# A two-block transformer kernel: nine steps of its hand-written order and bank assignment are moved

## The reference

```python
def first_block(x, ...):
    # layer A: chunked gated linear attention (GLA), 4 heads
    proj = rmsnorm(h) @ a_w_in                  # q 512, k 512, v 1024, gate 1024, glr 16
    gk = log_sigmoid(glr @ w_gk2 + b_gk) / 16
    bcum = cumsum(gk) in chunks of 64
    q_t, k_t, k_dec = q*exp(bcum), k*exp(-bcum), k*exp(b_last - bcum)
    h = h + (norm(tril(q_t @ k_t.T) @ v + q_t @ S) * silu(gate)) @ a_w_out
    h = h + relu(rmsnorm(h) @ w_up)**2 @ w_down      # 1024 -> 4096 -> 1024
    # layer B: sliding window attention, 16 query heads, 2 key heads, window 128
    h = h + swa(rmsnorm(h) @ b_w_q, rmsnorm(h) @ w_kv, bias = rel_table[bucket], sinks) @ b_w_out
    h = h + relu(rmsnorm(h) @ w_up)**2 @ w_down
    return rmsnorm(h, ln_final)

def second_block(x, p, ...):
    z = rmsnorm(x) @ w_in            # qa, ka, va, qb, kb, vb, gates ga, gb
    y_a = rope_attention(qa, ka, va) @ w_out_a
    y_b = dilated_attention(qb, kb, vb, rel_bias) @ w_out_b
    x = x + (sigmoid(ga + b) * y_a + sigmoid(gb + b) * y_b) @ w_out
    x = x + relu(rmsnorm(x) @ w_ff1)**2 @ w_ff2
    x = x + sigmoid(rmsnorm(x) @ w_ple_gate) * (p @ w_ple)
    return rmsnorm(x)
```

## Time and profile before

| | |
|---|---|
| time, median of 3 runs | 1019.68 us (1018.61 to 1027.45) |
| the profiled execution | 1019.38 us, of which the span of instructions is 1017.6 us |
| mean granted clock of TensorE | 0.993 |
| busy: PE, DVE, ACT, POOL | 990.9, 672.9, 492.8, 29.9 us |
| moved by DMA | 177.29 MB, 174 GB/s on average |

### The profile page before, as it was taken

The page is one execution under the profiler, slowest core; times in us unless marked ns, Lnnn a source line. Parts: engine busy times, 40 slices in busy tenths (PEclk is TensorE's granted clock), DMA queues, the critical chain, the costliest instruction groups (busy, mean ns, idle before and its releaser), DMA issues.

```text
span 1017.6 us, 13016 instructions
## 1 busy us (share of the span) xinstructions
PE 990.9 (97%) x5404; PEld 837.4 (82%) x5404; DVE 672.9 (66%) x931; ACT 492.8 (48%) x584; POOL 29.9 (3%) x56
## 2 busy tenths in 40 slices
PE   8989999999999999999999999999999999999997
PEld 7776888888888777888888889878878788888886
DVE  4765866656656985765656658975756585656665
ACT  4353444444445774544444455346553453444453
POOL 1000100000000000000000012000000000000001
PEclk9989999999999999999999999999999999999999
DMA  6752569655563325995455565344166465455551
GB/s 194 225 192 83 165 157 256 208 182 191 202 212 124 125 87 142 243 290 178 166 193 182 206 206 165 128 143 145 44 201 209 158 224 190 166 173 199 186 187 42
DMA packets 113100, 177.29 MB, mean 174 GB/s; under 512 B 4563, under 2 KB 75615, under 8 KB 113040
## 3 DMA queue, kind: packets, MB, share of 16 engines
q1 hardware_dynamic: 113040, 176.44, 55.0%
HBM read 174.60 MB, written 1.83 MB: 173 GB/s over the span
## 4 chain that ended last, share of the span: by engine, by line
PE 82%; DVE 9%; ACT 3%; DMA 3%; issue 1%; POOL 1%; SPq 1%; POOLq 0%; DVEq 0%; ACTq 0%
PE ps L285 79%; PE ps L289 3%; DVE wlo L1080 3%; DMA raw<-in_a_w_in 3%; DVE M L1088 2%; ACT M L1919 1%; DVE M L1080 1%; ACT whi L1922 1%; SPq L2600 1%; POOL st L2494 1%; DVE cc L1685 1%; DVE RR L1088 0%; DMA M<-in_ln_mix 0%; ACT M L1922 0%; DVE st L1641 0%
## 5 line engine op out<-in xcount | busy, mean ns | idle before, releaser
L285 PE MATMUL ps<-whi,RR 128*128 128x512 f32 (+1 forms) x1552 | 401.4, 390 | 1.6 <-DVE RR L1080 1.3
L1080 DVE TENSOR_TENSOR wlo<-raw,whi 128x1024 fp32r<-128x1024 f32 (+1 forms) x322 | 372.6, 1199 | 30.4 <-ACT whi L1922 30.0
L1922 ACT ACTIVATE whi<-raw 128x2048 fp32r<-128x2048 f32 (+2 forms) x162 | 302.6, 1871 | 179.3 <-PE ps L285 129.0
L285 PEld LDWEIGHTS ps<-whi,RR 128*128 128x128 f32 x1552 | 284.5, 189 | 61.5 <-issue 5.1
L285 PE MATMUL ps<-RR,whi 128*128 128x512 f32 (+1 forms) x1264 | 262.7, 352 | 5.3 <-DVE RR L1088 3.5
L285 PEld LDWEIGHTS ps<-RR,whi 128*128 128x128 f32 x1264 | 201.2, 190 | 34.2 <-issue 4.6
L285 PE MATMUL ps<-wlo,RR 128*128 128x512 f32 (+1 forms) x776 | 221.3, 387 | 0.9 <-DVE wlo L1080 0.9
L285 PEld LDWEIGHTS ps<-wlo,RR 128*128 128x128 f32 x776 | 144.3, 189 | 31.5 <-DVE wlo L1080 1.7
L1080 DVE TENSOR_TENSOR M<-M,ps 128x512 f32<-128x512 f32 x56 | 38.3, 686 | 168.1 <-ACT M L1922 164.7
L285 PEld LDWEIGHTS ps<-RR,wlo 128*128 128x128 f32 (+1 forms) x1016 | 138.5, 190 | 9.3 <-DVE wlo L1080 0.7
L285 PE MATMUL ps<-RR,wlo 128*128 128x256 f32 (+1 forms) x1016 | 144.9, 282 | 0.0
(11 more groups left out here) (94 smaller groups left out, 374.7 us busy)
## 6 DMA issues: line engine op xcount, KB each, us to landing
raw<-in_w_up SPq DMA_DIRECT2D x32, 1024.0 KB, 5.3
raw<-in_w_down SPq DMA_DIRECT2D x32, 1024.0 KB, 5.0
raw<-in_w_ff SPq DMA_DIRECT2D x32, 1024.0 KB, 5.2
raw<-in_w_in SPq DMA_DIRECT2D x23, 1024.0 KB, 5.2
raw<-in_a_w_in SPq DMA_DIRECT2D x11, 1024.0 KB, 8.4
raw<-in_a_w_out SPq DMA_DIRECT2D x4, 1024.0 KB, 5.0
raw<-in_b_w_q SPq DMA_DIRECT2D x4, 1024.0 KB, 5.0
raw<-in_b_w_out SPq DMA_DIRECT2D x4, 1024.0 KB, 5.0
```

The costliest lines, as they stand in the source:

```text
L285: return pe.matmul(out, lhsT, rhs, start=start, stop=stop, skip_group_check=True)
L1080: return dve.tensor_tensor(out, a, b, op)
L1922: return act.activation(out, in_, ACT.Copy, **k)
```

## The change

Nine places of the hand-written order are altered; the set of results is the same.

1. Start: PE warms up with 9 small products instead of 4, x's first half is transposed before the gain's transpose, which goes to bank 0, and its second half after five more warm-up products. SP loads the identity before x. ACT makes a small copy first, so its table is loaded ahead.
2. Bias rows: `line(i)` makes one bias row (on PE a product, on DVE its copy), and it is called from inside `gates()`: row 0 after gate 0, row 1 after gate 1, rows 2 and 3 after the next two steps. The stores of SP stay where they are.
3. `gates()` on DVE no longer yields between `kt` and `kd`, so `kd` comes before the low part of the next block.
4. The transposes of norm 2's quarters 0 and 1 take banks 4 and 5 instead of the next `misc()` banks.
5. `rows_scale(2)` is called before the key half, and the low part of a block (`take()`) before the copy of the scales on DVE.
6. In `window()` the low parts come before the shares.
7. The call of `early()` is also made at step 6 of the output projection, and `gemm_up` takes the bank pair of its second block when it reaches that block.
8. The tile `pT` takes bank 3.
9. On ACT the sigmoids of `SA` come after the rounding of the weights of `gemm_b(1024, 2)`.

```diff
--- before.py
+++ after.py
@@ -371,34 +371,30 @@
                 t = mm(b[:, i, T:2 * T], lo[:, k, 128 * i:128 * i + 128], hT[0][:, k, :], False, k == 7)
             return t
 
+
         blocks = []
         for f in range(0, n, 256):
             j, hi, lo = block(w[:, c0 + f:c0 + f + 256], 8, 256)
             tile = name + (f,)
             take(tile, *misc_pair())
-            blocks.append((tile, K.pair(tile, 512), j, hi, lo))
+            b = K.pair(tile, 512)
+            blocks.append((tile, b, j, hi, lo))
+            for i in range(2):
+                t = part(b, i, j, hi, lo, range(4) if hook else range(8))
+                if i == 0:
+                    if hook and f == 0:
+                        hook()
+                    yield
             if not hook:
-                for i in range(2):
-                    t = part(*blocks[-1][1:2], i, j, hi, lo, range(8))
-                    if i == 0:
-                        yield
                 t.then_inc(*K.filled(tile))
                 K.value["w_used", j] = K.full(tile)
                 yield
-        if hook:
-
-            for n_, (tile, b, j, hi, lo) in enumerate(blocks):
-                for i in range(2):
-                    part(b, i, j, hi, lo, range(4))
-                    if n_ == 0 and i == 0:
-                        hook()
-                        yield
-            for tile, b, j, hi, lo in blocks:
-                for i in range(2):
-                    t = part(b, i, j, hi, lo, range(4, 8))
-                t.then_inc(*K.filled(tile))
-                K.value["w_used", j] = K.full(tile)
-                yield
+        for tile, b, j, hi, lo in blocks if hook else []:
+            for i in range(2):
+                t = part(b, i, j, hi, lo, range(4, 8))
+            t.then_inc(*K.filled(tile))
+            K.value["w_used", j] = K.full(tile)
+            yield
 
     def gemm_b(name, w, c0, n, xT, ready, pairs=None):
 
@@ -435,7 +431,7 @@
 
     def norm_turn(s, k2):
         tile = ("nt", s, k2)
-        b = take(tile, 2 * (k2 - 2) if s in (1, 2, 3, 5) and k2 > 1 else misc())
+        b = take(tile, 2 * (k2 - 2) if s in (1, 2, 3, 5) and k2 > 1 else 4 + k2 if s == 2 else misc())
         for j in range(2):
             k = 2 * k2 + j
             for c in range(2):
@@ -546,14 +542,16 @@
         for _ in range(n):
             mm(K.banks[:, 3, 0:128], V.S["ones"][:, :], V.S["ones"][:, :], True, True)
 
-    spin(4)
+    spin(9)
+    norm_early(0)
     tile = ("g", 0)
-    b = take(tile, misc())
+    b = take(tile, 0)
     for w in due(K.dma("id"), K.dma("g0")):
         pe.wait_ge(*w)
     tr(b[:, 0:16], V.M[0:16, 0:128]).then_inc(*K.filled(tile))
     spin(5)
-    norm_rest(0)
+    for k2 in (2, 3):
+        norm_turn(0, k2)
 
 
 
@@ -576,7 +574,9 @@
     tr(b[:, 0:60], V.M[0:60, 15000:15128]).then_inc(*K.filled(tile))
 
     tab, sel = V.S["tab"], V.S["sel"]
-    for i in range(4):
+
+    def line(i):
+
         tile = ("br", i)
         b = take(tile, misc())
         for w in due(K.dma("tab", 1), K.at("tab_end"), K.dma("sel")):
@@ -597,8 +597,11 @@
                 h = 2 * h2 + j
                 t = mm(b[:, j * 256:j * 256 + 256], V.S["gk2"][:, h * 128:h * 128 + 128], V.glr, True, True)
             t.then_inc(*K.filled(tile))
-            yield
-        for _ in range(4):
+            line(h2)
+            yield
+        for i in range(4):
+            if i < 2:
+                line(2 + i)
             yield
         while count["qk"] < 4:
             yield
@@ -728,8 +731,8 @@
     t = q_part(1, range(4, 8))
     t.then_inc(*K.filled(("q2",)))
     K.value["w_used", jq] = K.full(("q2",))
+    rows_scale(2)
     kv_part(0, range(4, 8)).then_inc(*K.filled(("kk",)))
-    rows_scale(2)
     kv_part(1, range(4, 8)).then_inc(*K.filled(("vt",)))
     K.value["w_used", jk] = K.full(("vt",))
 
@@ -1033,7 +1036,7 @@
     project("po", A["w_out_2"][0], 5, "ty", lambda: turn_parts("ty", V.SB, 1, K.at("mix", 512)), V.tyT)
 
     pT = oB
-    b = take(("pT",), misc())
+    b = take(("pT",), 3)
     for w in due(K.dma("p")):
         pe.wait_ge(*w)
     for j in range(2):
@@ -1361,11 +1364,13 @@
                 t = ts(bc[:, h * 256:h * 256 + 256], K.bank(tile)[:, j * 256:j * 256 + 256], G[:, 64 + h:65 + h], None,
                        ALU.add, None)
             t.then_inc(*K.emptied(tile))
+            line(h2)
             yield
         for w in due(K.empty(("gate", 0)), K.empty(("gate", 1))):
             dve.wait_ge(*w)
         stt(e1, bc, -1.0, bc, ALU.mult, ALU.max).then_inc(*K.up("g_abs"))
         low = step(ts(bc, bc, 0.0, None, ALU.min, None))
+        line(2)
         yield
         for w in due(K.at("g_ln"), low):
             dve.wait_ge(*w)
@@ -1373,6 +1378,7 @@
         for w in due(d):
             dve.wait_ge(*w)
         d = step(ts(e1, e1, 1.0 / 16.0, None, ALU.mult, None))
+        line(3)
         yield
         for w in due(d, K.at("scan_one")):
             dve.wait_ge(*w)
@@ -1517,6 +1523,7 @@
     squares(2, *xs_free(2), *all_x(K, 2))
     kv_lows(2, 3)
     diagonals(2)
+    take()
     for w in due(K.full(("rbt", 2))):
         dve.wait_ge(*w)
     dve.tensor_copy(RB[:, 0:256], K.bank(("rbt", 2))[:, 0:256]).then_inc(*K.emptied(("rbt", 2)))
@@ -1527,7 +1534,6 @@
             t = tt(V.KT[64 * half:64 * half + 64, g, :], K.bank(("kk",))[64 * g:64 * g + 64, 0:256],
                    RB[64 * g:64 * g + 64, 0:256], ALU.mult)
     t.then_inc(*K.emptied(("kk",)))
-    take()
 
     def cc(p):
         return S["cc"][:, 32 * (p % 3):32 * (p % 3) + 32]
@@ -1576,10 +1582,10 @@
         for i in range(11):
             if i < 8:
                 soft(i)
+            if 3 <= i:
+                lows(i - 3)
             if 0 < i < 9:
                 shares(i - 1)
-            if 3 <= i:
-                lows(i - 3)
             yield
 
     def halves(n):
@@ -1601,6 +1607,8 @@
         if at > 4:
             n, c = (at - 5) // 2, (at - 5) % 2
             add_x(("pr", n, c), n, c)
+        if at == 6:
+            early()
 
     mlp(1, 3, 4)
 
@@ -2066,6 +2074,10 @@
             act.wait_ge(*w)
         copy(V.hi[:, 0, h], V.raw[:, 0, h]).then_inc(*K.up("w_hi", (0, 0) if i == 0 else 0))
 
+
+    for w in due(K.at("ones")):
+        act.wait_ge(*w)
+    copy(st[:, 63:64], S["ones"][:, 0:1])
     norm_early(0)
     first_high(0)
     norm_turn(0, 2)
@@ -2408,13 +2420,12 @@
         for w in due(K.empty(("gb", f, 0)), K.empty(("gb", f, 1))):
             act.wait_ge(*w)
         actf(V.SB[:, :, f:f + 512], V.SB[:, :, f:f + 512], ACT.Sigmoid).then_inc(*K.up("sig", ("b", f)))
+    run_all((gemm_b(1024, 2, lambda f, m, c: None), 1))
     for w in due(*[K.empty(("ga", f, c)) for f in (0, 512) for c in range(2)], K.full(("fv", 7))):
         act.wait_ge(*w)
     for c in range(2):
         t = actf(V.SA[:, c, :], V.SA[:, c, :], ACT.Sigmoid)
     t.then_inc(*K.up("sig", "a"))
-
-    run_all((gemm_b(1024, 2, lambda f, m, c: None), 1))
     g = gemm_b(1024, 8, lambda f, m, c: None)
     for _ in range(6):
         next(g)
@@ -2614,9 +2625,10 @@
 
     xd = A["x"].rearrange("a (c p) d -> p (a c) d", p=128)
     for n in range(2):
+        if n == 0:
+            load("id", 0, S["ident"][:, :], A["c_ident"])
         load("x%d" % n, 0, V.x[:, :, n * 512:n * 512 + 512], xd[:, :, n * 512:n * 512 + 512])
         if n == 0:
-            load("id", 0, S["ident"][:, :], A["c_ident"])
             load("g0", 0, M[0:16, 0:128], rows(A["ln_mix"]))
         w = K.blocks[0][0][512 * n:512 * n + 512, :] if K.blocks else A["a_w_in"][0][0:512, 0:256]
         load("w0" if n else "w_first", 0, V.raw[:, 0, 1024 * n:1024 * n + 1024].rearrange("p (k n) -> p k n", k=4),
```

## The result

| | before | changed |
|---|---|---|
| median of 18 runs | 1018.83 us | 1012.64 us (1009.90 to 1017.36) |
| ratio | | 0.9935, 95% interval 0.9918 to 0.9952 |
| profiled execution, span | 1017.6 us | 1008.1 us |

The change gives back 6.6 us (1018.83 x 0.0065, interval 4.9 to 8.4); the median lies 0.4 from the forecast of 1012.2. The profiled execution of the changed kernel, 1009.9, is the fastest of its 18, so its trace shows 9.5 us less than the trace of before. Its mean granted clock is 0.997, where the median of the 18 is 0.995: an estimate from these two is that some 2 of the 2.7 us between it and the median are time at the lower clock.

A forecast was written before the change was run, and what follows sets the result against it. TensorE is busy 97% of the span, so only about 27 us idle and lower-clock time can return. Terms -0.4 - 2.66 - 0.95 - 1.04 - 1.61 - 0.56 = -7.2 on 1019.4 give 1012.2 us; range 1006.5 to 1017, own forecast 1009.8 to 1013.4 (0.42).

The forecast's parts named there:

- Start: Kernel start, x's transposes first: 0.65 us off SP's later loads (bounds 0 to 0.65), nothing on PE.
- Bias rows, bank wait: First gates: bias row 1 waits 2.1 us for bank 5 until DVE reads it, with a clock dip of +1.7.
- Bias rows, B7: Weight block 7's load, behind the last bias-row store: issued 50.5, not 36.38; lands 59.8; PE waits 2.7 us.
- rival 2: PE's 2.7 us wait for weight block 7 brings the lower clock, +2.7: 1014.9 us; chance 0.20.
- no dip: At PE's 2.7 us wait for weight block 7: clock stays up, as the wait is nearer 2.46 (none) than 3.35.
- rival 1: Weight block 7's load is cheap, landing 5.0 us after issue: 1008.8 us, without the new dip 1006.7; chance 0.27.
- kd ahead: First block, before the scores: decayed keys precede B8's low part, 8.1 us after B7's landing; 3.35 wait becomes 0.6.
- Net of the region: Start, bias rows and key product together, up to the first scores: 71.5 against 71.89, net -0.4 us.
- Norm 2: Transposes in banks 4 and 5 (-1.56), row scales ahead (+0.85, -0.77), softmax-chain wait of 1.18 gone: -2.66 us together.
- The four late waits: PE waits at 368.33, 398.12, 803.16 and 754.06 (and just behind) vanish: -0.95, -1.04, -1.61, -0.56 us.
- rival 4: Small waits refill: each of five gains ends at the next semaphore, under half of 6.8 left: 1016 to 1019.5; chance 0.06.

The follow-up runs named there:

- the late edits alone: Kernel before with only lows before shares, early lows at step 6, pT in bank 3 and ACT's weights before the second sigmoids: 1014.39 us, ratio 0.9944.

## Why the prediction was right, step by step

**Start.** I took 0.65 off the loads and nothing off PE. PE's first product came 1.0 earlier, B4 landed 3.1 earlier (28.93). The step failed in size: the low part of B0 came 1.2 earlier, not 0.65, the trace of before held a slow issue on SP (1.4 us for the selection matrix, 0.37 in the changed kernel) that I read as fixed, and PE, which I took as full from 11.5 on, began its products earlier. By itself the edit does not show in the time.

**Bias rows, bank wait.** Right as a mechanism, 2.1 forecast, 0.36 in the changed kernel's trace, since B4 came early; 1.05 and 1.81 in the two traces where it came later. The dip behind it, +1.7, was absent there and present with waits of 0.35, 0.50, 1.05 and 1.81. So I over-sized the wait. The dip was there in four of the six traces that have this wait, and cost 1.5 in three of them and 3.1 in the fourth.

**Bias rows, B7.** The chain of reasoning held: issue 46.84 (forecast 50.5), 10.70 to landing (9.3), landing 57.54 (59.8). PE's wait was 4.25, not 2.7, because PE itself arrived 3.7 us earlier than I had walked it; the dip behind it, rival 2's, was there (59.5 to 63.3 at 0.56) and also in the other traces with waits of 2.77, 3.06 and 4.33. The scores hang on B7's landing and not on PE's arrival: the landing was 2.3 earlier than forecast, the dip cost some 1.6, and the forecast wait of 0.6 for kd did not come. So rival 2's mechanism happened and the time still fell into my own range: that part is luck. **The part of the prediction that failed in kind is this "no dip", with the reason that a wait of 2.46 had left the clock at 1.00**: that was one lucky trace; in five others the same wait brought the lower clock. A sum of rival 1 was wrong too: without the new dip kd, at 63.6, would have held PE, which gives 1007.8 and not 1006.7.

**kd ahead.** Right: no wait for it in any kernel with the edit once B7 was there (6.4 by itself at the scores, 6.1 expected by its two parts). **Net of the region.** -0.4 was forecast, the two traces give -2.0. It is the kd edit's gain (6.4 at the scores by itself) less what the rows cost there (4.8 by themselves). One pair of traces overstates how well this is known. The start of the kernel before also stands in the trace of the late edits alone, with the scores at 69.97, and that of the changed kernel in the traces without the scales' and the banks' edit, at 69.63 and 70.68. By all five the net is about -0.9 (70.9 against 70.1 on average), between forecast and first reading.

**Norm 2.** -2.66 forecast, -2.50 in the trace: 1.55 from the banks (1.56 forecast), 0.69 lost at bank 6 (0.85), 0.95 net for the scales. What I missed is the dip of 1.4 to 1.6 that the banks edit also prevents, in five of the six traces with that wait.

**The four late waits.** -0.95, -1.04, -1.61, -0.56, in sum -4.2; in the trace -2.25 and -2.96, in sum -5.2, and -5.7 (3.7 to 7.7) by themselves. Right, slightly small: the last two places gave 1.84 and 1.12 instead of 1.61 and 0.56; what the rest of it is was not traced.

**Not foreseen:** in eight of ten experiments PE waits in the second MLP for weights that are held up by the scratch reads, 0.45 to 1.82 for the longest wait, and so part of a gain further ahead is given back. This is rival 4's thought, at one place only. That the sum came out so near is in part luck: the trace says -9.5, the runs -6.6, and the forecast -7.2 lies between.

## What to carry to other kernels

A load that many engines wait for must not stand behind stores that wait for small copies, whatever the stores' own size: look at every queue in which a moved step's outputs are issued. Before spreading a group of small matmuls, price what waits behind each of them on the other engines; here the run cost one dip of 1.7, and spreading it cost 6 to 7, because a weight load stood behind the last matmul's store. With that load moved ahead of the last store, both orders took the same time. A dip behind a wait that one trace lacks is not excluded: read several executions before a clock of 1.00 is used as a rule.

## What the runs showed of the hardware

A megabyte issued right behind one fresh store of 4 rows by 16 by 511 elements landed after 9.24, 9.52, 10.70, 10.80 and 10.81 us (five traces), behind four stores issued within 3 us after 17.6, 17.9, 18.0, 18.2 and 19.2 (five traces), while loads elsewhere have a median of 5.0. So one fresh store costs 4.2 to 5.8 us, and the four 12.6 to 14.2 together, though part of them had drained before the load was issued.

The windows of the changed kernel show what the price is. From 28 to 31 only weights move, at 36 to 39 the first store (16 rows) and the beginning of the second, and from 40 to 46.8 only stores of 4 rows:

```profile
28.00:31.00 3.00, 3.00 (x17) 1.84 (x16) 0.11 (x1) 1.91 (x1) 0.00 (x0) 1.00 1.05 385
36.00:39.00 3.00, 3.00 (x25) 2.92 (x24) 2.81 (x3) 0.17 (x1) 0.00 (x0) 1.00 0.90 102
40.00:46.80 6.80, 6.80 (x39) 5.26 (x39) 5.00 (x8) 3.40 (x3) 0.00 (x0) 1.00 0.23 25
```

The last number is GB/s, the one before it the busy share of the 16 DMA engines. A store of 4 rows, 131 KB, takes 5.2 us at 25 GB/s, which is the price above; 0.23 of 16 engines is 3.7. In the trace of before, too, the rate was 36 GB/s at a share of 0.25 from 41 to 44, although B7 had been issued at 36.38. That reads as B7's part on the stores' engines waiting for them; a store of the same bytes in another shape, which would test it, was not run.

The Trainium skill's page "DMA: Bandwidth & Descriptors", section "Why a DMA increments its semaphore by 16 and not by 1", lets a copy of 4 rows use 4 of 16 engines, and the busy share of 0.23 agrees. The estimate of 1.2 us that the prediction worked out with a quarter of the page's 436 GB/s does not hold: the store moved at 25 GB/s, a quarter of what that estimate took, and the measurement decides.

The clock fell to its lower level behind PE waits of 2.46 (at norm 2, five of six traces), 2.77, 2.99, 3.06, 3.35, 4.25 and 4.33, and not behind one of 1.65. It fell behind the four bias rows in a run in all five traces that have them (0.50 at 30.8 to 34.2 in before, 0.57 to 0.59 at 30 to 34 in the others). It also fell behind waits of 0.35 to 1.81 with a gate product ahead and a bias row behind, in four of six traces; in the two without, the waits were 0.36 and 0.32. A single trace therefore tells a dip's cost (1.3 to 3), not whether it will be there.
The Trainium skill's page "TensorE: Matmul & The Clock Gate", section "Why this matters for your kernels", warns of long idle gaps between bursts of matmuls. The falls behind 3.35, 4.25 and 4.33 agree with it. Those behind 2.46 to 2.99 came at gaps shorter than the one that the page names, and those at 0.35 to 1.81, with thin products around them, at much shorter ones: there the measurements decide.
